# Hybrid decoder layer on one core: moving one head group's scores, the edge products and one PSUM copy inside the mix loop

## The reference, cut to what matters

```python
h = rmsnorm(x, mix_norm)
sq, sk, sv, gq, gk, gv, gg, glr, mq = split(h @ w_in)
y_swa = swa_attention(...)     # 8 heads, window 128, sinks, relative bias
y_gla = gla(...)               # 4 heads of gated linear attention
y_mem = memory_attention(...)  # 4 heads against 256 memory tokens
x = x + concat(y_swa, y_gla, y_mem) @ w_out
```

## Time and profile before

| | |
|---|---|
| median of 3 runs | 1687.62 us (1686.52 to 1688.25) |
| the profiled execution, its own time | 1687.72 us |
| its span, first to last instruction | 1685.7 us |
| PE busy | 1670.3 us (99%) |
| DVE / ACT / POOL busy | 1111.7 / 728.9 / 554.0 us |
| blocks 1 to 6 of the mix | 855.22 to 943.12 us of the span |

### The profile page before, as it was taken

One profiled execution on the slowest core, in us unless ns is written; L12 is line 12 of the kernel. 1 busy time (PEld: TensorE's weight loads), 2 busy tenths in 40 slices (PEclk: granted clock), 3 DMA queues, 4 the chain that ended last, 5 costly groups with the idle time before them and its releaser, 6 DMA issues.

```text
span 1685.7 us, 25103 instructions
## 1 busy us (share of the span) xinstructions
PE 1670.3 (99%) x8399; PEld 1373.1 (81%) x8399; DVE 1111.7 (66%) x1581; ACT 728.9 (43%) x1378; POOL 554.0 (33%) x471
## 2 busy tenths in 40 slices
PE   9999999999999999999989999999999999999999
PEld 7888888888888889888766787888888888888887
DVE  7965555555489598458888945985555555569654
ACT  6533333333344464333378723443333333334442
POOL 0544445544130134022266422354444444310000
PEclk9999999999999999999999999999999999999999
DMA  7342222233774532120100123133333223574434
GB/s 214 81 144 94 100 100 93 100 108 118 260 257 145 162 95 87 63 88 13 38 2 2 64 75 137 39 107 107 119 114 109 93 93 106 191 275 148 147 98 165
DMA packets 101790, 191.73 MB, mean 114 GB/s; under 512 B 11539, under 2 KB 14068, under 8 KB 101708
## 3 DMA queue, kind: packets, MB, share of 16 engines
q1 hardware_dynamic: 100624, 188.50, 33.0%
q0 software_dynamic: 848, 2.10, 0.9%
q10 hardware_dynamic: 236, 0.06, 0.0%
HBM read 139.76 MB, written 50.86 MB: 113 GB/s over the span
## 4 chain that ended last, share of the span: by engine, by line
PE 95%; DVE 2%; DMA 1%; issue 0%; ACT 0%; SPq 0%; POOLq 0%; POOL 0%; DVEq 0%; ACTq 0%
PE ps L57 30%; PE ps L59 30%; PE ps L58 30%; DVE A_T L2111 2%; PE ps L1879 1%; PE ps L1916 1%; PE ps L1864 1%; PE ps L1755 1%; DMA xT<-in_x 1%; PE ps L1931 0%; PE ps L1832 0%; PE ps L1902 0%; DMA down_raw<-act_dram 0%; PE ps L1413 0%; PE ps L1415 0%
## 5 line engine op out<-in xcount | busy, mean ns | idle before, releaser
L523 DVE TENSOR_TENSOR ring<-w_raw,ring 128x512 fp32r<-128x512 f32 x240 | 239.1, 1011 | 218.5 <-ACT ring L518 218.4
L57 PE MATMUL ps<-hiT,ring 128*128 128x512 f32 x672 | 261.5, 389 | 0.0
L59 PE MATMUL ps<-hiT,ring 128*128 128x512 f32 x672 | 261.4, 389 | 0.0
L58 PE MATMUL ps<-loT,ring 128*128 128x512 f32 x640 | 249.0, 389 | 0.0
L57 PE MATMUL ps<-down_ring 128*128 128x512 f32 x616 | 239.9, 389 | 0.4 <-DVE down_ring L901 0.4
L58 PE MATMUL ps<-down_ring 128*128 128x512 f32 x616 | 239.6, 389 | 0.0
L59 PE MATMUL ps<-down_ring 128*128 128x512 f32 x616 | 239.6, 389 | 0.0
L57 PE MATMUL ps<-hiB,ring 128*128 128x512 f32 x576 | 224.8, 390 | 0.3 <-DVE loB L388 0.3
L59 PE MATMUL ps<-hiB,ring 128*128 128x512 f32 x576 | 224.1, 389 | 0.0
L518 ACT ACTIVATE ring<-w_raw 128x512 fp32r<-128x512 f32 x240 | 150.6, 628 | 169.8 <-PE ps L59 165.1
L897 ACT ACTIVATE down_ring<-down_raw 128x512 fp32r<-128x512 f32 x176 | 108.7, 629 | 225.6 <-DMA down_raw<-act_dram 181.5
(11 more groups left out here) (302 smaller groups left out, 3005.7 us busy)
## 6 DMA issues: line engine op xcount, KB each, us to landing
down_raw<-act_dram SPq DMA_DIRECT2D x154, 256.0 KB, 2.7
w_raw<-in_w_gate SPq DMA_DIRECT2D x88, 256.0 KB, 3.0
w_raw<-in_w_up SPq DMA_DIRECT2D x88, 256.0 KB, 3.1
act_dram<-actT SPq DMA_DIRECT2D x88, 256.0 KB, 2.0
act_dram<-act SPq DMA_DIRECT2D x66, 256.0 KB, 2.0
wd<-in_w_down SPq DMA_DIRECT2D x44, 256.0 KB, 5.0
wd_mirrored<-in_w_down SPq DMA_DIRECT2D x33, 256.0 KB, 4.3
p_raw<-in_w_proj SPq DMA_DIRECT2D x15, 512.0 KB, 3.7
```

The lines of the kernel that those rows point to most:

```text
L57: nc.tensor.matmul(out, w_hi, x_hi, start=first, stop=False, skip_group_check=resumed)
L58: nc.tensor.matmul(out, w_hi, x_lo, start=False, stop=False, skip_group_check=resumed)
L59: return nc.tensor.matmul(out, w_lo, x_hi, start=False, stop=last, skip_group_check=resumed)
L523: nc.vector.tensor_tensor(ring[:, e % RING, 1, :], op_source(e), ring[:, e % RING, 0, :].bitcast(F32), ALU.subtract).then_inc(op_ready, 1)
```

## The change

Three moves within the order of one block; no operation is added, removed or resized. On PE, `scores(1, n+1)` goes from behind `gla_out(n)` to ahead of `turn(1, n)`, right behind the spans. On ACT, `o_copy(n)` goes behind `exps(0, n+1)`. On DVE, `gate_edges` for the next block is done at the end of a block, ahead of `denominators(0, n+1)`, and no longer at the next block's start. The last block has no next one, so on PE and ACT it stays as it is.

```diff
@@ mix_tensor
+                if more:
+                    scores(pe, 1, n + 1)
                 turn(1, n)
                 if more:
                     turn_k_hat(n)
                 gla_out(n)
                 if more:
-                    scores(pe, 1, n + 1)
                     key_values(n)
@@ mix_scalar
-                o_copy(n)
                 if more:
                     exps(0, n + 1)
-                    if n:
-                        out_gate(n)
+                o_copy(n)
+                if more and n:
+                    out_gate(n)
                 pt_copy(2, n)
@@ mix_vector
                 more = n + 1 < NB
-                if n:
-                    gate_edges(dve, n)
                 if not more:
                     gate_out(n - 1)
                 denominators(dve, 1, n)
@@
                     if n:
                         gate_out(n - 1)
+                    gate_edges(dve, n + 1)
                 else:
```

## The result

The changed kernel took 1695.36 us (median of 6 runs, 1694.04 to 1696.33), the kernel before 1687.93 us (6 runs). The ratio is 1.0049, with a 95% interval from 1.0039 to 1.0060: 0.5% slower. The profiled execution took 1695.11 us with a span of 1693.2, 7.5 us more than before.

A forecast was written before the change was run, and what follows sets the result against it. PE's products and ACT's run, ACT's later, were taken to bound each block from second turn to memory values. 9.1 for six blocks, -1.3 for block 0 and -0.3 for block 7 made +7.5, or 1695.2 us; range 1691 to 1701.

The forecast's parts named there:

- block 0's term: Block 0: scores start earlier and memory values come earlier, -1.3 us; -0.6 if the half clock comes there again.
- Two chains: Second turn to memory values: PE's products and ACT's run nearly level, ACT's later; a later turn moves ACT's run wholly.
- Rival (b): ACT catches up and only PE's chain counts: +3.6 us, 1691.3 us; chance 0.12.
- The scores: Blocks 1 to 6: scores wait for the decays, so the second turn slips; 11.55 us, +9.1 after what is won back.
- The two small waits won back: ACT's waits at the sinks' exponential and memory unit's copy vanish: 0.22 + 0.20 = 0.42 us a block, 2.45 in six.
- Copy and edges: Linear output's copy on ACT costs nothing; edges at the block's end show by 0.1 to 0.2 us, hidden by PE's slip.
- Block 7: Block without next scores: edges moved from its start free DVE for the copies into A_T earlier, -0.3 us.
- Rival (a): The clock falls in three to six blocks, 1.0 us each on top: 1698 to 1702 us; chance 0.29.

The follow-up runs named there:

- the wait alone: Kernel before, scores in their old place, with the second turn also waiting for the decays: 1692.44 us, ratio 1.0039.
- longer decays: Big decay exponential cut into four in blocks 1 to 7: 1699.65 us in the changed kernel, 1686.96 us in the kernel before.
- the first block only: Kernel before with scores directly behind the spans in block 0 alone, and edges, copy and tanh moved: 1686.24 us, ratio 0.9995.
- the variant: Changed kernel with scores behind second turn and turned keys, except block 0's, which stay directly behind the spans: 1685.22 us, ratio 0.9990.
- the scores behind the turn: Changed kernel with scores put behind second turn and turned keys, ahead of the linear output; timed twice: 1685.57 us, then 1685.56 us.

## Why the prediction was right

The forecast was 1695.2 us, the measured median 1695.36. The six blocks came out by the mechanism that was forecast; block 0's term came out right on a ground that doesn't hold.

**What bounds.** Two chains, nearly level, from the second turn to the memory values, ACT's the later: shown by the tanh taken out of ACT's run, which shortened each block by its own 0.31, and PE's 0.56 of wait at the memory values. Rival (b), PE's chain alone, would have given 15.4 a block; it was 16.03, for the 16.0 of the sum.

**The scores.** Term for term: a wait of 1.52 for a forecast 1.53; ACT's idle 2.35 for about 2.3; 0.05 for 0.06 at each hand-over; +9.1 for six blocks, as summed. That the wait for the decays is the cause, and not an earlier place as such, is shown from three sides: the wait alone costs +5.3, a place behind the turn costs nothing, and longer decays cost their 0.17 a block here and nothing in the old order. The other 3.8 are the scores' 1.06 between decays and turn less 0.42 won back, six times.

**The two small waits won back.** The sinks' exponential and the memory unit's copy now follow their neighbours without a gap. I had 0.42 for them. From the turned keys' copy to the memory values it was 897.91 - 892.64 = 5.27 in block 3 before and is 900.96 - 896.11 = 4.85 after: 0.42 less.

**Copy and edges.** Nothing and 0.1 to 0.2, hidden by PE's slip: so it was. Alone, without that cover, they cost 0.06 and 0.09 a block. Block 7 gained 12.50 - 12.23 = 0.27 from block 6's memory values to its own, for the forecast 0.3 (954.53 - 942.03 before, 962.09 - 949.86 after).

**Block 0: the right number on the wrong ground.** I gave the new place -1.3 (my own sum, 852.7 against 854.13, would be -1.4). The memory values there did come at 852.86. But the old order does it in 853.06 - 841.66 = 11.40, in the execution with the edges alone, against 852.86 - 841.37 = 11.49 after the change. What differed was the clock: in the earlier trace rows it fell in block 0, which then took 854.13 - 841.22 = 12.91. The rows of the levels in the kernel before, the changed one and the edges alone, and of the memory values in the last:

```profile
841.22 1.79 PE L1864 MATMUL ps<-hi_raw 32*128 32x64 f32 x56 [0.35 <-DVE ggT L1653]
...
841.37 1.79 PE L1864 MATMUL ps<-hi_raw 32*128 32x64 f32 x56 [0.35 <-DVE ggT L1653]
...
841.66 1.79 PE L1864 MATMUL ps<-hi_raw 32*128 32x64 f32 x56 [0.35 <-DVE ggT L1653]
...
853.06 1.09 PE L1931 MATMUL ps<-glu,mv 128*64 128x128 f32 x16 [0.80 <-ACT glu L2022]
```

So the step that failed is the term of block 0: I took one execution's fall as part of the kernel before. The place itself is worth about +0.1, and 1.4 hangs on whether the clock falls. At a full clock in both, the change sums to 9.1 + 0.1 - 0.3 = 8.9 us, and the scores' move alone, which lacks the 0.3, to 9.2. Sorted by clock, the latter measured +8.6 among executions with a mean of 1.000 (1694.58, two of them, against 1686.03, six) and +8.8 among those under it (1696.02, three, against 1687.23, fifteen). The 7.5 of the two profiled executions, one with a fall and one without, is too little for that comparison, and the ratio's interval, 6.6 to 10.1 us, holds both.

Whether the new place makes falls in block 0 rarer, so that part of the -1.3 belongs to it, or whether that was luck, is open. Executions under 1.000 are common in the kernel before, 53 of the 84 timed beside the experiments, and two of six in the changed one. For the place speaks that PE's gap there becomes 1.52, and that none of the 22 executions of the two versions with only this gap (the first block only, and the variant) stood under 1.000. Against it, the scores behind the turn kept a gap of 1.86 and 1.88 in their traces and had only three of 11 under 1.000 each time. Only one execution of each has a trace.

**Rival (a), the clock.** In the profiled execution it held in all six blocks behind gaps of 1.52. It isn't out of the world: one of five executions with the wait alone stood at 0.996 and took 4.5 us more; it has no trace. My 1702 for six falls at 1.0 should have been 1701. The advice of the Trainium skill that I cited ("TensorE: Matmul & The Clock Gate", section "Why this matters for your kernels") warns only of longer gaps. These six blocks agree with it; block 4 of the longer decays, where the clock fell behind a gap of 1.70, does not, and the measurement decides.

## What to carry to other kernels

Before moving work into a hole of an engine that goes in order, ask when its own last condition is met, not only how long the hole is; here a hole of 0.73 us would have taken work that could start only after it had closed. A wait that had been met 1.5 us before in the old place cost nothing there and 0.9 us a block in the new. And compare a stage of two traces at the same clock before giving a difference to the edit.

## What the runs showed of the hardware that I had not expected

The length of the gap doesn't settle whether the clock falls. Behind a gap of 1.87 us it fell to 0.50 in block 0 of the kernel before; behind 1.86 in the same place it held in the execution with the edges alone:

```profile
847.50 0.63 PE L1879 MATMUL ps<-ident,Pg 128*128 128x128 f32 x4 [1.86 <-DVE A_T L2111]
...
848.76 1.13 PE L1755 MATMUL ps<-kT,qT 64*128 64x256 f32 x8
```

The scores took 1.13 there, not 1.91. With the scores behind the turn it fell behind 1.86 in one profiled execution and held behind 1.88 in the other. What decides it is not shown. A fall in this stage costs 1.4 to 1.6 us, more than the better place of the scores wins at the same clock (0.6 to 0.9). Cutting an exponential over 1024 columns into four cost 0.17 us, a third of what I had estimated.
